# Half of a small product moved to an earlier norm, attention's half-array products regrouped, and an odd entry in other banks

## What is computed

```python
# first block
h = rms_norm(x, g_mix_pre); u, q, k, v = split(h @ w_in)
y = concat(pool_mixer(u), attention(q, k, v, bias)) @ w_out     # 8 heads of 64: the first attention
x = x + rms_norm(y, g_mix_post)                                 # the first post-norm
x = x + rms_norm(conv_ffn(rms_norm(x, g_ffn_pre)), g_ffn_post)  # the second post-norm
x = x + (p @ w_ple) * sigmoid(x @ w_ple_gate)                   # the per-layer product, p: 256 x 256
# second block, even layer
y = concat(conv_mixer, window_attention_with_sinks) @ ev_w_out  # 8 heads of 64: the second attention
x = layer_norm(ALPHA * x + y); x = layer_norm(ALPHA * x + swiglu(x))
# second block, odd layer: od_w_in is the "odd entry"
y = concat(gated recurrence (GLA), latent attention (MLA)) @ od_w_out
x = layer_norm(ALPHA * x + y); x = layer_norm(ALPHA * x + swiglu(x))
```

## Time and profile before

| | us |
|---|---|
| median of three runs | 905.91 (905.78 to 905.96) |
| the profiled execution | 905.97 |
| its span, first to last instruction | 904.2 |
| TensorE's first product of the first feed-forward | starts at 96.75 |
| its first product of the gate | starts at 293.66 |
| its last filler of the second attention | about 399.9 to 402.8 |
| VectorE busy, ScalarE busy, GpSimd busy | 675.3, 510.1, 120.8 |

### The profile page before, as it was taken

One profiled execution on the slowest core, in us unless ns is written; L12 is line 12 of the kernel. 1 busy time (PEld: TensorE's weight loads), 2 busy tenths in 40 slices (PEclk: granted clock), 3 DMA queues, 4 the chain that ended last, 5 costly groups with the idle time before them and its releaser, 6 DMA issues.

```text
span 904.2 us, 18130 instructions
## 1 busy us (share of the span) xinstructions
PE 890.6 (99%) x6750; PEld 839.8 (93%) x6750; DVE 675.3 (75%) x1113; ACT 510.1 (56%) x755; POOL 120.8 (13%) x78
## 2 busy tenths in 40 slices
PE   8999999999999999999999999999999999999997
PEld 6977899999999999999999999999899999999996
DVE  5975797777777866889766686789787886668665
ACT  7355644434435645977555555567397756555552
POOL 1000000000000023002132230300120022324003
PEclk9999999999999999999999999999999999999999
DMA  8863275565564655435655555434434475565541
GB/s 314 327 225 109 73 243 180 182 203 173 180 202 147 201 194 165 140 118 187 201 180 176 189 182 186 149 133 140 131 106 145 145 221 187 170 201 175 173 139 47
DMA packets 44147, 156.82 MB, mean 173 GB/s; under 512 B 5082, under 2 KB 5573, under 8 KB 43973
## 3 DMA queue, kind: packets, MB, share of 16 engines
q1 hardware_dynamic: 42336, 152.17, 51.0%
q10 hardware_dynamic: 1317, 2.43, 0.7%
q0 software_dynamic: 448, 1.59, 0.5%
HBM read 155.11 MB, written 1.06 MB: 173 GB/s over the span
## 4 chain that ended last, share of the span: by engine, by line
PE 91%; DVE 5%; ACT 2%; issue 1%; DMA 1%; SPq 0%; POOL 0%; DVEq 0%; POOLq 0%; ACTq 0%
PE ps L401 21%; PE ps L403 21%; PE ps L402 21%; PE ps L444 5%; PE ps L446 5%; PE ps L445 5%; PE ps L524 1%; PE ps L548 1%; DVE w_lo L1394 1%; PE ps L414 1%; PE ps L421 1%; PE ps L415 1%; PE ps L526 1%; PE ps L525 1%; PE ps L845 1%
## 5 line engine op out<-in xcount | busy, mean ns | idle before, releaser
L401 PE MATMUL ps<-op_hi,w_hi 128*128 128x258 f32 (+1 forms) x1330 | 377.3, 284 | 1.3 <-DVE w_lo L1394 0.7
L403 PE MATMUL ps<-op_hi,w_lo 128*128 128x258 f32 (+1 forms) x1330 | 375.4, 282 | 0.0
L402 PE MATMUL ps<-op_lo,w_hi 128*128 128x258 f32 (+1 forms) x1330 | 374.8, 282 | 0.0
L1394 DVE TENSOR_TENSOR w_lo<-raw,w_hi 128x1024 fp32r<-128x1024 f32 x224 | 288.5, 1314 | 22.5 <-ACT w_hi L1017 19.9
L1017 ACT ACTIVATE w_hi<-raw 128x1024 fp32r<-128x1024 f32 x224 | 231.2, 1052 | 69.2 <-PE ps L403 35.6
L401 PEld LDWEIGHTS ps<-op_hi,w_hi 128*128 128x128 f32 x1330 | 251.2, 189 | 5.0 <-issue 1.9
L402 PEld LDWEIGHTS ps<-op_lo,w_hi 128*128 128x128 f32 x1330 | 251.7, 189 | 2.0
L403 PEld LDWEIGHTS ps<-op_hi,w_lo 128*128 128x128 f32 x1330 | 251.3, 189 | 0.0
L1010 ACT ACTIVATE w_hi<-raw 128x1024 fp32r<-128x1024 f32 x60 | 63.4, 1057 | 61.6 <-PE ps L403 31.4
L401 PE MATMUL ps<-mix_hi,w_hi 128*128 128x256 f32 x336 | 96.1, 286 | 1.0 <-DVE mix_lo L1559 1.0
L403 PE MATMUL ps<-mix_hi,w_lo 128*128 128x256 f32 x336 | 94.6, 281 | 0.0
(11 more groups left out here) (290 smaller groups left out, 1094.6 us busy)
## 6 DMA issues: line engine op xcount, KB each, us to landing
raw<-in_stream SPq DMA_DIRECT2D x284, 512.0 KB, 3.7
x<-in_x SPq DMA_DIRECT2D x4, 256.0 KB, 5.4
bias<-bias_rows POOLq DMA_DIRECT2D x1, 1024.0 KB, 8.6
work<-in_last_norm SPq DMA_DIRECT2D x1, 1024.0 KB, 5.7
result<-y SPq DMA_DIRECT2D x4, 256.0 KB, 2.0
y<-in_spans ACTq DMA_DIRECT2D x1, 640.0 KB
bias<-bias_rows POOLq DMA_DIRECT2D x1, 512.0 KB, 11.7
proj<-in_gmask ACTq DMA_DIRECT2D x1, 512.0 KB
```

Source lines behind the costliest of these rows:

```text
L401: pe.matmul(o, wh, xh, start=start, stop=False, **kw)
L402: pe.matmul(o, wh, xl, start=False, stop=False, **kw)
L403: return pe.matmul(o, wl, xh, start=False, stop=stop, **kw)
L1394: m = dve.tensor_tensor(w_lo[:, s, :], raw[:, s, :], fp(w_hi[:, s, :]), ALU.subtract)
```

## The change

- **Stream**: the two units of `w_ple` are rearranged by output: the first holds the outputs 0 to 3 for both halves of p, the second the outputs 4 to 7. The first comes ahead of the first feed-forward, the second stays ahead of the gate.
- **First post-norm** (`ple_with_turned_rows`): in place of the three constant products, 12 products of the per-layer product ahead of the transposes, 3 between those of the two token halves, and 9 behind. Results lie in banks 7 and 0; ScalarE copies them to `ple_kept`. The split of p moves into the first entry. ScalarE and VectorE split one more weight unit ahead of the norm. The feed-forward's first two chunks go to banks 2 and 3, its statistic to bank 4.
- **Second post-norm**: 18 products ahead of the transposes, 6 behind. x is signalled by chunk instead of by pair.
- **First and second attention**: values go to banks 4 and 5; a transposition no longer waits for a mix, but for the copy of the pair before; values wait for a mix and for the reads of the scores. On TensorE `values(0)` stands right behind `scores(3)`, and the later transposes right ahead of values. VectorE's and ScalarE's lists are reordered.
- **Odd entry**: its first two chunks lie in banks 4 and 5, and the wait for the four pieces moves to the third.
- **GLA**: two of the eight input chunks of one `out_chunk` move behind the spread. **MLA**: ScalarE makes the hi part of the first pair's result.

```diff
+            def ple_part(o, c, k):
+                s, w = take(), slice((2 * c + k) * P, (2 * c + k) * P + P)
+                return three(o, w_hi[:, s, w], w_lo[:, s, w], p_hi[:, k, :], p_lo[:, k, :], k == 0, k == 1)
+            def ple_with_turned_rows():
+                pe.wait_ge(S["p_split"], 1)
+                for c in range(2):
+                    for k in range(2):
+                        m = ple_part(chunk(7, c), c, k)
+                m.then_inc(S["ple_done"], 1)
                 for t in range(2):
                     if t:
-                        idle_turn(0)
+                        ple_part(chunk(0, 0), 2, 0)
                     for f in range(2):
                         pe.wait_ge(*((S["rows_dve"], t + 1) if t == f else (S["rows_act"], t + 1)))
...
+                ple_part(chunk(0, 0), 2, 1)
+                ple_part(chunk(0, 1), 3, 0)
+                m = ple_part(chunk(0, 1), 3, 1)
+                given(m)
...
-            def pair_turn(g, mixed):
+            def pair_turn(g):
                 pe.wait_ge(S["pair_scaled"], g + 1)
-                pe.wait_ge(S["mix_ready"], mixed)
+                if g:
+                    pe.wait_ge(S["pair_copied"], g)
...
-            def pair_values(g, v):
+            def pair_values(g, v, read, mixed):
                 pe.wait_ge(S["pair_copied"], g + 1)
+                pe.wait_ge(S["pair_read"], read)
+                pe.wait_ge(S["mix_ready"], mixed)
...
             def swa_values(p):
-                pair_values(4 + p, lambda e, t: vtok[:, t, e * 64:e * 64 + 64])
+                pair_values(4 + p, lambda e, t: vtok[:, t, e * 64:e * 64 + 64], 8 if p else 7, 12 + p)
...
-            pair_turn(4, 12)
+            pair_turn(4)
             swa_scores(2)
             mix_filler(2, 12)
+            mix_filler(3, 12, 0)
+            pair_turn(5)
+            swa_scores(3)
             swa_values(0)
-            mix_filler(3, 12, 0)
-            pair_turn(5, 13)
-            swa_scores(3)
             mix_filler(3, 12, 1)
+            pair_turn(6)
             swa_values(1)
             mix_filler(4, 13)
-            pair_turn(6, 14)
             mix_filler(5, 14, 0)
+            pair_turn(7)
             swa_values(2)
             mix_filler(5, 14, 1)
-            pair_turn(7, 15)
             mix_filler(6, 15, 0)
...
                 if c == 0:
-                    pe.wait_ge(S["z_ready"], 8)
-                    first_chunks(bank(0, 0, SEQ + 2), bank(1, 0, SEQ + 2), 5, *raw_operand)
+                    first_chunks(bank(odd_bank(0), 0, SEQ + 2), bank(odd_bank(1), 0, SEQ + 2), 5, *raw_operand)
                     square_mean(6)
                 if c == 2:
+                    pe.wait_ge(S["z_ready"], 8)
...
-            out_chunk(chunk(6, 0), mix_hi, mix_lo)
+            out_chunk(chunk(6, 0), mix_hi, mix_lo, ks=range(6))
             pe.wait_ge(S["gla_copied"], 1)
             spread([(2 * h + t, 2 + h // 2, h % 2 * SEQ + t * P) for h in range(GLA_H) for t in range(2)])
+            out_chunk(chunk(6, 0), mix_hi, mix_lo, ks=range(6, NCH))
...
@@ ScalarE, pair_attention @@
                     step()
                     pair_copy(g + 2)
                 step()
-                step()
                 pair_copy(g + 3)
+                step()
                 step()
                 step()
...
@@ ScalarE @@
             pair_attention(0, moba_values_ready)
+            split_hi()
             row_squares()
             scaled_row(0, 0, 1)
             scaled_row(0, 1, 0)
-            operand_hi(x, "x_ready", gain="g_ffn_pre")
-            act.wait_ge(S["late_loaded"], 16 * len(late_consts))
-            act.activation(p_hi[:], pt[:], ACT.Copy).then_inc(S["p_hi_done"], 1)
+            act.wait_ge(S["ple_done"], 1)
+            act.activation(ple_kept[:, 0:2, :], bank2(7), ACT.Copy).then_inc(S["ple_evac"], 1)
+            operand_hi(x, gain="g_ffn_pre")
+            unit.n += 1
+            unit_done()
+            act.activation(ple_kept[:, 2:4, :], bank2(0), ACT.Copy).then_inc(S["ple_evac"], 1)
             feed_forward(True)
...
             pair_copy(8)
             step()
+            act.wait_ge(S["pair_summed"], 9)
+            act.activation(mix_hi[:, 4:6, :], ps[:, 4:6, 0:SEQ], ACT.Copy).then_inc(S["mla_mix_hi"], 1)
             pair_copy(9)
...
@@ VectorE, pair_shift @@
+                if g in (3, 7):
+                    dve.wait_ge(S["pair_summed"], g - 2)
...
@@ VectorE, pair_attention: before / after @@
                 step()
                 pair_shift(g + 2, tile(2), sink)
                 pair_scale(g + 1, sink)
+                pair_scale(g + 2, sink)
+                step()
                 pair_mix(g, turned)
-                step()
                 pair_shift(g + 3, tile(3), sink)
-                pair_scale(g + 2, sink)
+                step()
+                pair_scale(g + 3, sink)
                 pair_mix(g + 1, turned)
-                if sink:
-                    pair_scale(g + 3, sink)
-                step()
-                if not sink:
-                    pair_scale(g + 3, sink)
+                step()
                 pair_mix(g + 2, turned)
-                step()
                 step()
                 pair_mix(g + 3, turned)
...
@@ VectorE, MLA @@
-            mla_mix(0)
+            dve.wait_ge(S["mla_mix_hi"], 1)
+            dve.tensor_tensor(mix_lo[:, 4:6, :], ps[:, 4:6, 0:SEQ], fp(mix_hi[:, 4:6, :]), ALU.subtract
+                              ).then_inc(S["mix_ready"], 2)
```

More of the change, by code:

```diff
@@ L222, in pair, with turned_apart, gate_bank, odd_bank @@
             return t[:, 2 * i:2 * i + 2, :]
+        def turned_apart(c):
+            return chunk(4 + c // 2, c % 2) if c < 6 else chunk(1, c % 2)
+        def gate_bank(c):
+            return (4, 5, 2, 3, 0, 1, 2, 3)[c]
+        def odd_bank(c):
+            return 4 + c if c < 2 else c % 4
         def bank2(b):
@@ L426, in first_chunks, with out_chunk @@
                     out_chunk(p, hi, lo)
-            def out_chunk(o, hi=op_hi, lo=op_lo, half=None):
+            def out_chunk(o, hi=op_hi, lo=op_lo, half=None, ks=range(NCH)):
                 s = take()
-                for k in range(NCH) if half is None else range(4 * half, 4 * half + 4):
+                for k in ks if half is None else range(4 * half, 4 * half + 4):
                     w = slice(k * P, k * P + P)
                     m = three(o, w_hi[:, s, w], w_lo[:, s, w], hi[:, k, :], lo[:, k, :], k == 0, k == NCH - 1)
-                if half != 0:
+                if k == NCH - 1:
                     given(m)
@@ L592, in down @@
                     (in_chunk if shifted and not final else row_chunk)(h_hi[:, c, :], h_lo[:, c, :], first, last)
-                j, start, stat = hidden.n, 4 if shifted else 0, 0 if shifted else 2
+                j, start, stat = hidden.n, 4 if shifted else 2, 0 if shifted else 4
                 first_chunks(bank(start, 0, n), bank(start + 1, 0, n), operand, hi, lo)
@@ L600, in feed_forward @@
                 out_chunk(bank(6, 0, n), hi, lo, half=1)
+                if not shifted:
+                    pe.wait_ge(S["ple_evac"], 2)
                 out_chunk(bank(7, 0, n), hi, lo)
@@ L754, in _ @@
                 if c == 0:
-                    first_chunks(chunk(0, 0), chunk(1, 0), 2, mix_hi, mix_lo)
+                    first_chunks(chunk(gate_bank(0), 0), chunk(gate_bank(1), 0), 2, mix_hi, mix_lo)
+                    pe.wait_ge(S["x_chunk"], 16)
                 elif c > 1:
-                    out_chunk(chunk(c % 4, 0), mix_hi, mix_lo)
+                    out_chunk(chunk(gate_bank(c), 0), mix_hi, mix_lo)
             for c in range(18):
@@ L979, in _ @@
             gla_filler(2, 20)
-            pair_turn(8, 20)
+            pe.wait_ge(S["mix_ready"], 20)
+            pair_turn(8)
             gla_filler(3, 20, 0)
@@ L983, in _ @@
             gla_filler(3, 20, 1)
[L984 removed]
+            pair_turn(9)
             mix_filler(4, 22)
@@ L1058, in operand_piece, with operand_hi @@
                 act.activation(pair(dst, i), pair(src, i), ACT.Copy).then_inc(S["norm_hi"], 2)
-            def operand_hi(src, ready, gain=None):
-                for i in range(4):
+            def operand_hi(src, gain=None):
+                for c in range(NCH):
                     if gain is None:
-                        operand_piece(mix_hi, src, ready, i)
-                    else:
-                        for c in (2 * i, 2 * i + 1):
-                            act.wait_ge(S["x_chunk"], c + 1)
-                            act.activation(op_hi[:, c, :], src[:, c, :], ACT.Copy, scale=vcol(gain, c)
-                                           ).then_inc(S["norm_hi"], 1)
+                        act.wait_ge(S["x_chunk"], NCH + c + 1)
+                        m = act.activation(mix_hi[:, c, :], src[:, c, :], ACT.Copy)
+                    else:
+                        act.wait_ge(S["x_chunk"], c + 1)
```

(4 more changed lines are left out.)

106 lines of the change are left out of this document (50 added, 56 removed).

## The result

The changed kernel takes 910.66 us in the median (910.00 to 911.03) against 905.93 for the kernel before (905.78 to 906.18): 1.005 times as long, 95% interval 1.0036 to 1.0065. The forecast was 908.5 with a range up to 910.8, so sign and range hold, the range by 0.14 us only: two of the four runs (910.86 and 911.03) lie above it, and its upper part was there for rival (a), the falling clock. The time is that of rival (a), 0.8 us above the 909.9 given for it. The profiled execution took 910.86 us with a span of 909.0.

A forecast was written before the change was run, and what follows sets the result against it. TensorE, busy nearly the whole span, was taken as the bound. The terms 0.4 - 2.45 + 0.2 + 5.6 - 0.5 + 0 - 0.7 = +2.55 on 905.97 us gave 908.5 us, range 905.0 to 910.8.

The forecast's parts named there:

- rival (a): Second attention: the 5.0 us pause lets TensorE's granted clock fall, costing 1.4 us more, 909.9 us in all; chance 0.32.
- First post-norm: More per-layer products and a late row square start the feed-forward later: +0.4 us, bounds 0 and +0.8.
- the walk: First post-norm, followed link by link: transposes wait twice for 0.1 to 0.2 us, feed-forward starts 0.6 late.
- the give-back: First post-norm: the square means, which waited for VectorE's sums before, give back 0.2 us of the late start.
- The four waits: TensorE waits before MLA's projection, at the odd entry, in GLA and the second attention; together 2.7 us, the most removable.
- Second post-norm: Transposes start 0.35 us earlier and 6 products stand behind them for 24: -2.45 us, bounds -2.8 and -2.0.
- First attention: Joining half-array groups saves 0.2 us, VectorE's new order costs 0.4 of wait: net +0.2, bounds -0.4 and +0.9.
- Second attention: VectorE's mix of pair 1 behind the fourth weight split makes TensorE wait: +5.6 us, bounds +4.5 and +6.2.
- The walk over the two queues: Second attention, VectorE and ScalarE in list order: waits of 1.25 us at values 1 and 5.0 from 392.1 to 397.1.
- Odd entry, GLA, MLA: Odd entry: first chunk's wait goes, -0.5 us. GLA: wait won, then lost, 0. MLA: cast on ScalarE shortens wait, -0.7.

The follow-up runs named there:

- six constant products: The changed kernel with six constant products of 384 columns, read by nobody, put into the second attention's pause of 4.9 us: 908.63 us.
- the better kernel: The changed kernel with, in both attentions, VectorE's mix 0 and shift 3 ahead of the third weight split, mix 1 and scaling 3 ahead of the fourth: 901.84 us.
- two constant products: The changed kernel with two constant products, read by nobody, in the second attention's pause behind filler 4: 909.15 us median of six runs.

## Why the prediction was right, and where it wasn't

- **First post-norm**, +0.4 forecast, +0.13 measured. The start of the feed-forward slipped by 0.49 (4.89 for 4.40), near the 0.6 of the walk; the give-back that I set at 0.2 was 0.36. The ends 0 and 0.8 hold it. The four waits said to bound what can be won, 2.7 us, left out the 0.42 that the earlier trace rows shows here; the sum doesn't use that bound.
- **Second post-norm**, -2.45 and -2.38. The transposes start 2.57 us behind the first per-layer product (286.67 to 289.24), with a wait of 0.25 for the second scaling, where I had them at 2.5. Undoing both norms together costs 2.12 by the experiment.
- **First attention**, +0.2 and +0.35. Both its parts were right in kind: 0.2 won by joining, 0.5 lost to the order where I had 0.4. The pace of the earlier trace rows was the whole argument for the 0.2. The Trainium skill (TensorEngine Tiling (Array Packing), Key Properties) says that a change of tiling mode drains TensorE; the trace agrees in so far as one joined pair of groups saves 0.2 in each attention. Whether that is one side of 0.2 or two of 0.1 isn't shown.
- **Second attention**, +5.6 and +8.06. The walk over the two queues is right almost link by link. It put the pause at 5.0 us and the wait ahead of it at 1.25; they are 4.89 and 1.26. The walk's end of the pause, 397.1 less the 1.9 that both kernels differ by up to there, is 395.2; the trace has 395.32. With the clock kept up the whole kernel takes 908.63 us (six constant products) where 908.5 was forecast, so the queue part of the sum is right. That VectorE and ScalarE took up their lists in order was enough to forecast it; the 4.96 us for which VectorE stood idle ahead of a mix that was ready show it.
- **The step that failed** is the one where I left the clock up, the term for rival (a) put at nothing in the sum. I gave the fall 0.32 and its absence 0.44, on the ground that one fall at the end of a trace is no rule. The trace had it at 3.7 us after the last product, and the pause that I forecast was longer than that; nothing in the rows spoke for its staying up. That 910.66 is still within the range is owed to rival (a), not to the sum. The measured fall came 3.1 us into the pause (4.89 less the 1.8 at the lower level). The Trainium skill (TensorE: Matmul & The Clock Gate, Why this matters for your kernels) warns of idle gaps between bursts of products, and by that rule rival (a) stood ahead; the trace agrees with it.
- **The size of rival (a)**, 1.4 and 2.3. I took it from the twelve constant passes at the start, 5.73 us where I allowed 4.9. The windows of the trace of before give that stretch a granted clock of 1.00:

```profile
0.00:5.00 5.00, 3.73 (x7) 2.12 (x8) 0.00 (x0) 1.49 (x2) 0.98 (x11) 1.00 0.53 146
```

  So no row shows the lower level there, and why these passes are slow stays open (twelve of them in the filled pause took 4.14). The 1.4 had no measured fall under it, and its nearness to the 2.3 is no merit of the working. What is lost here can be worked out from the spacing: 256 columns 0.213 us apart instead of 0.12, and six transposes 1.41 us to the next start instead of 0.75, run at 0.53 to 0.56 of the pace, which over 5.1 us makes 2.2 to 2.4 us, beside the 2.29.
- **Odd entry, GLA, MLA**: -0.5, 0 and -0.7; undone one by one they give 0.48, -0.03 and 0.80. For GLA the sum was right and the place was not: I expected a wait of 0.5 at the transposes of MLA's first pair, and 0.45 of the 0.58 are given back at the scores of the second pair, 0.11 ahead of those transposes.

The pieces of the better kernel add up: 2.12 + 0.48 + 0.80 - 0.03, and 0.2 and 0.55 of the two attentions, make 4.1 of the 4.2 us by which it is under the kernel before. Two things stay open: why the runs with two constant products fall into two groups, if it is the clock, and why the constant passes at the start are slow at a granted clock of 1.00. No run here separates causes for either.

## What to carry to other kernels

Where independent work is listed behind an item that waits for another engine, price it by that wait: here one group listed behind one split made 4.1 us of wait and 2.1 of lost clock, and with two such groups listed ahead of their splits no wait of over 0.2 us came in their place. After finding a new pause, ask how long it is against the longest at which the trace shows the clock still up; where it may fall, add its price (2.3 us for a pause of 4.9 here), or put products into it. Removing a wait of 0.6 us is worth nothing until the next wait behind it has been read.

## What was not expected of the hardware

That a pause of TensorE seems to have no single outcome: by times and mean clocks, a stand of 2.94 us (in the profiled run) let the granted clock fall in three of six runs, 1.65 us in none of nine, 4.89 us in all of four; of the falls only one, at 4.89, has a trace. Where the fall can be placed it came 3.1 us into the stand, and 3.7 us at the end of the trace of before. And that the cost lies behind the pause: 1.8 us of the lower level lay in it and cost nothing, 5.1 us lay in unbroken products behind it and cost 2.3.
